# Reordering the first weight chunks of a two-layer diffusion backbone: the first projection chunk before half of the modulation

## What is computed

```python
mod = silu(c) @ w_ada[l] + b_ada[l]                 # 6 x 1024: shift, scale, gate for each half
h = rms_norm(x, norm_g[l, 0]) * (1 + sc_m) + sh_m
q, k, v, u, vm, bg, cg, hx = split(h @ w_in[l])     # 1024 x 2816
y = concat([attention(q, k, v), gating_mlp(u, vm), short_conv(bg, cg, hx)]) @ w_out[l]
x = x + gt_m * rms_norm(y, norm_g[l, 1])
h = rms_norm(x, norm_g[l, 2]) * (1 + sc_f) + sh_f
f = swiglu(h) if l == 0 else moe_swiglu(h)          # layer 1: top 2 of 8 experts
x = x + gt_f * rms_norm(f, norm_g[l, 3])
```

## Time and profile before

| | us |
|---|---|
| median of 3 runs | 1576.52 (1573.6 to 1576.85) |
| the profiled execution's own time | 1577.02 |
| its span, first to last instruction | 1575.2 |
| PE busy (matmul) | 1533.6, 97% of the span |
| DVE busy, ACT busy | 1019.3 (65%), 872.4 (55%) |
| chain that ended last, by engine | PE 89%, DVE 4%, DMA 3%, ACT 2% |

### The profile page before, as it was taken

The page is one execution under the profiler, slowest core; times in us unless marked ns, Lnnn a source line. Parts: engine busy times, 40 slices in busy tenths (PEclk is TensorE's granted clock), DMA queues, the critical chain, the costliest instruction groups (busy, mean ns, idle before and its releaser), DMA issues.

```text
span 1575.2 us, 26693 instructions
## 1 busy us (share of the span) xinstructions
PE 1533.6 (97%) x11239; PEld 1251.7 (79%) x11239; DVE 1019.3 (65%) x943; ACT 872.4 (55%) x889; POOL 178.6 (11%) x196
## 2 busy tenths in 40 slices
PE   5999999999999999999999999999999999999997
PEld 4787788888888888787888888888888878878876
DVE  1437573333323644667888888898888976666667
ACT  2535452222322545546777777777777764654555
POOL 3111100000000400013102030200303000002000
PEclk9999999999999999999999999999999999999999
DMA  9886425667665573145999999999999997778782
GB/s 325 309 278 177 128 82 162 222 222 247 227 244 205 156 237 121 56 158 204 383 384 385 376 376 385 369 379 377 383 377 373 384 360 256 267 277 303 255 331 84
DMA packets 215027, 426.23 MB, mean 271 GB/s; under 512 B 22272, under 2 KB 63520, under 8 KB 214272
## 3 DMA queue, kind: packets, MB, share of 16 engines
q1 hardware_dynamic: 200448, 397.99, 71.1%
q0 software_dynamic: 12640, 19.54, 4.2%
q10 hardware_dynamic: 1808, 6.86, 1.1%
HBM read 419.11 MB, written 20.87 MB: 279 GB/s over the span
## 4 chain that ended last, share of the span: by engine, by line
PE 89%; DVE 4%; DMA 3%; ACT 2%; SPq 1%; issue 0%; ACTq 0%; DVEq 0%
PE ps L1714 25%; PE ps L1716 25%; PE ps L1715 25%; PE ps L2283 3%; PE ps L1755 2%; PE ps L2249 1%; ACT whi L799 1%; PE ps L2316 1%; DVE wlo L1177 1%; DMA raw<-in_w_in_dram 1%; DMA raw<-in_w_ada_dram 1%; DVE x L1268 1%; PE ps L1903 1%; SPq L595 1%; PE ps L1887 1%; PE ps L1872 1%
## 5 line engine op out<-in xcount | busy, mean ns | idle before, releaser
L1177 DVE TENSOR_TENSOR wlo<-raw,whi 128x2048 fp32r<-128x2048 f32 x327 | 746.6, 2291 | 316.3 <-ACT whi L799 262.1
L799 ACT ACTIVATE whi<-raw 128x2048 fp32r<-128x2048 f32 x327 | 626.7, 1918 | 440.0 <-PE ps L1716 200.1
L1714 PE MATMUL ps<-whi,xhi 128*128 128x512 f32 (+1 forms) x1352 | 534.3, 395 | 5.5 <-DVE wlo L1177 5.1
L1716 PE MATMUL ps<-whi,xlo 128*128 128x512 f32 (+1 forms) x1352 | 522.3, 386 | 0.0
L1715 PE MATMUL ps<-wlo,xhi 128*128 128x512 f32 (+1 forms) x1352 | 521.8, 386 | 0.0
L1714 PEld LDWEIGHTS ps<-whi,xhi 128*128 128x128 f32 x1352 | 254.0, 188 | 63.3 <-issue 10.7
L1716 PEld LDWEIGHTS ps<-whi,xlo 128*128 128x128 f32 x1352 | 253.9, 188 | 52.7 <-issue 0.2
L1715 PEld LDWEIGHTS ps<-wlo,xhi 128*128 128x128 f32 x1352 | 254.4, 188 | 47.2
L1714 PE MATMUL ps<-whi,hhi 128*128 128x512 f32 x484 | 192.2, 397 | 0.0
L1716 PE MATMUL ps<-whi,hlo 128*128 128x512 f32 x484 | 188.8, 390 | 0.0
L1715 PE MATMUL ps<-wlo,hhi 128*128 128x512 f32 x484 | 188.6, 390 | 0.0
(11 more groups left out here) (262 smaller groups left out, 1096.9 us busy)
## 6 DMA issues: line engine op xcount, KB each, us to landing
raw<-in_w_moe_gu_dram SPq DMA_DIRECT2D x352, 512.0 KB
raw<-in_w_moe_d_dram SPq DMA_DIRECT2D x176, 512.0 KB
raw<-in_w_ada_dram SPq DMA_DIRECT2D x96, 512.0 KB
raw<-in_w_in_dram SPq DMA_DIRECT2D x44, 512.0 KB
raw<-in_w_ffn_gu_dram SPq DMA_DIRECT2D x44, 512.0 KB
raw<-in_w_ffn_d_dram SPq DMA_DIRECT2D x22, 512.0 KB
raw<-in_w_out_dram SPq DMA_DIRECT2D x16, 512.0 KB
bias<-rpb_rows POOLq DMA_DIRECT2D x32, 96.0 KB, 6.1
```

The source lines that it names most:

```text
L799: act.activation(whi[m % SPL][:, :], raw[n % RING][:, :], ACT.Copy).then_inc(s_hi, 1)
L1177: dve.tensor_tensor(wlo[n % RING][:, :], raw[n % RING][:, :], whi[NTH[n] % SPL][:, :].bitcast(F32), ALU.subtract).then_inc(s_lo, 1)
L1714: pe.matmul(out, a_hi, w_hi, start=start, stop=False)
L1716: return pe.matmul(out, a_lo, w_hi, start=False, stop=stop)
```

## The change

The first pairs go in the order 0, 2, 1, 3, and W6 follows directly behind pair 2, so that the shift and scale of k-tiles 0 to 3 come first. `x` is loaded after two chunks. The columns are made in two halves (`first_columns`), with a semaphore of their own, `s_modh`. On PE the products of pairs 1 and 3 move into W6, behind its first token tile. The later pairs follow W7 (4), W0 (5 and 6), W1 (7), W2 (8), W3 (9). `gvb`, `ws` and `bs` wait in addition until ACT has split W7 (`s_hi` 2); `rpb_rows`, `ck`, `cv` and `wcb` go behind the bias row of pair 6, which waits until DVE has made pair 4's gate. `repeated` moves to another address, and ACT's wait for `s_rows` falls away. The dummy matmuls become 12, 3 and 22 in place of 6, 6, 6, 3 and 8.

Stream order after: pair 0, pair 2; W6; pair 1, pair 3; W7; pair 4; W0; pairs 5, 6; W1; from there as before.

The diff, cut: left out are the renamings by which the first pairs' row buffers, banks and counts go by place (`place_of`) and not by pair.

```diff
-X_AFTER = 4
+X_AFTER = 2
...
-ADA_AFTER = [{p: [HEAD + p] for p in range(MIXER - HEAD)}, {1: [MIXER], 2: [MIXER + 1]}]
+HEAD_ORDER = [0, 2, 1, 3]
+ADA_AFTER = [{1: [4], 2: [5, 6], 3: [7], 4: [8], 5: [9]}, {1: [MIXER], 2: [MIXER + 1]}]
...
-    out = [("ada", 0, j) for j in range(2 * HEAD)]
-    out.insert(2 * HEAD - 2, ("win", 0, WIN_SEQ[0]))
+    out = [("ada", 0, 2 * i + h) for i in HEAD_ORDER for h in range(2)]
+    out.insert(HEAD, ("win", 0, WIN_SEQ[0]))
...
-    return first + 3 if n == first else n if first < n <= first + 2 else n + 1
+    return first + 5 if n == first else n if first < n <= first + 4 else n + 1
...
+def place_of(l, i):
+
+    return HEAD_ORDER.index(i) if l == 0 and i < HEAD else i
...
+        repeated = at("repeated", 48128, [P, 2 * KW * GW])
         qT = at("qT", 33792, [P, 4, NT * P])
...
                     pool.wait_ge(s_tr, KT)
-                    pool.wait_ge(s_rep, 1)
-                    pool.dma_start(rpb_rows.rearrange("l r q j -> (l r) (q j)"),
-                                   repeated[0:7 * NH * DEPTH, :]).then_inc(s_rows, 16)
+                    pool.wait_ge(s_hi, 2)
...
+                else:
+                    brow(l, 6)
+                    pool.wait_ge(s_rep, 1)
+                    pool.dma_start(rpb_rows.rearrange("l r q j -> (l r) (q j)"),
+                                   repeated[0:7 * NH * DEPTH, :]).then_inc(s_rows, 16)
...
-                    for i in range(6, MIXER):
+                    for i in range(7, MIXER):
...
-                upto(n_next)
-                act.wait_ge(s_modc, 2 * l + half + 1)
+                if s == 0:
+                    upto(PLACE["win", 0, WIN_SEQ[0]])
+                else:
+                    upto(n_next)
+                    act.wait_ge(s_modc, 2 * l + half + 1)
                 for kt in range(0, KT, 2 if s == 3 else 1):
+                    if s == 0 and kt == 4:
+                        upto(n_next)
+                    if s == 0 and kt % 4 == 0:
+                        act.wait_ge(s_modh, kt // 4 + 1)
...
-                        if l == 0 and p == 1 and t == 0:
-                            act.wait_ge(s_rows, 16)
...
+
+            def first_columns(h):
+
+                dve.wait_ge(s_colmm, 2 * h + 2)
+                dve.wait_ge(s_gcol, 16 * 2 * DEPTH)
+                k = slice(4 * h, 4 * h + 4)
+                shift, scale = [ps[:, 7, COLUMNS_AT + 16 * i:COLUMNS_AT + 16 * i + 16]
+                                .rearrange("p (k g) -> p k g", g=2)[:, k, :] for i in range(2)]
+                dve.tensor_copy(modc[:, 0, k, :], shift)
+                for g in range(2):
+                    ins = dve.scalar_tensor_tensor(out=modc[:, 1, k, g], in0=scale[:, :, g], scalar=1.0,
+                                                   in1=gcol[:, 0, 0, k], op0=ALU.add, op1=ALU.mult)
+                ins.then_inc(s_modh, 1)
+                if h:
+                    ins = dve.sem_inc(s_modc, 1)
...
+                    if s == 0 and kt == 4:
+                        for i in HEAD_ORDER[2:]:
+                            ada(0, i)
+                        first_columns(1)
+                        upto(PLACE["win", 0, WIN_SEQ[1]])
...
-            for i in range(HEAD):
-                ada(0, i)
-                if i == HEAD - 3:
-                    scaled(0, 0, 0)
-                if i == HEAD - 2:
-                    upto(PLACE["win", 0, WIN_SEQ[0]])
-            mod_columns(0, 0)
+            ada(0, HEAD_ORDER[0])
+            scaled(0, 0, 0)
+            ada(0, HEAD_ORDER[1])
+            first_columns(0)
+            upto(PLACE["win", 0, WIN_SEQ[0]])
...
-                for i in range(HEAD):
-                    if i == 1:
-                        pe.wait_ge(s_const, N_CONST)
-                    if i == HEAD - 1:
-                        for kt in range(4):
-                            turn_x(0, kt)
-                        ada_turn(0, HEAD - 2)
-                        for kt in range(4, KT - 1):
-                            turn_x(0, kt)
-                        warm(6, 4)
-                    ada(0, i)
-                    if 0 < i < HEAD - 1:
-                        ada_turn(0, i - 1)
-                        warm(6, 4)
+                ada(0, HEAD_ORDER[0])
+                pe.wait_ge(s_const, N_CONST)
+                ada_turn(0, HEAD_ORDER[0])
+                warm(12, 4)
+                for kt in range(KT - 1):
+                    turn_x(0, kt)
+                ada(0, HEAD_ORDER[1])
                 warm(3, 4)
-                ada_turn(0, HEAD - 1)
-                warm(8, 4)
+                ada_turn(0, HEAD_ORDER[1])
+                warm(22, 4)
                 turn_x(0, KT - 1)
+
+            def rest_of_head(turn):
+
+                for i in HEAD_ORDER[2:]:
+                    if turn:
+                        ada_turn(0, i)
+                    else:
+                        ada(0, i)
...
+                            if l == 0 and p == 0 and t == 1 and i == 0:
+                                rest_of_head(True)
+                        if l == 0 and p == 0 and t == 0:
+                            rest_of_head(False)
```

More of the change, by code:

```diff
@@ L192, in build @@
         pr = at("pr", 0, [P, NT, D_IN])
-        repeated = at("repeated", 16384, [P, 2 * KW * GW])
+        repeated = at("repeated", 48128, [P, 2 * KW * GW])
         qT = at("qT", 33792, [P, 4, NT * P])
@@ L280, in build @@
         s_modc = sem("s_modc")
+        s_modh = sem("s_modh")
         s_ss = sem("s_ss")
@@ L447, in ada_out @@
             if l == 0 and i < HEAD:
-                return ps[:, 5 + i % 2, NT * P:NT * P + P]
+                return ps[:, 5 + place_of(l, i) % 2, NT * P:NT * P + P]
             return ps[:, 6 if (l, i) in ADA_IN_FFN else 5 + i % 2, 0:P]
@@ L620, in brow @@
             def brow(l, i):
-                if ADA_B * l + i >= 2:
-                    pool.wait_ge(s_modr, ADA_B * l + i - 1)
+                p = place_of(l, i)
+                if ADA_B * l + p >= 2:
+                    pool.wait_ge(s_modr, ADA_B * l + p - 1)
                 for g in range(2):
-                    pool.dma_start(brow_of[g:P:32, i % 2, :],
+                    pool.dma_start(brow_of[g:P:32, p % 2, :],
                                    b_ada[l, 512 * i:512 * i + 512].rearrange("(j n) -> j n", j=4)
-                                   ).then_inc(s_brow[i % 2], 16)
+                                   ).then_inc(s_brow[p % 2], 16)
             def norm_row(l, j):
@@ L637, in _ @@
             chain(pool.memset(grow[:, :, :], 0.0))
-            brow(0, 0)
-            brow(0, 1)
+            brow(0, HEAD_ORDER[0])
+            brow(0, HEAD_ORDER[1])
             const = Chain(pool, s_const)
@@ L695, in _ @@
                 else:
-                    brow(l, 2)
-                    brow(l, 3)
+                    brow(l, HEAD_ORDER[2])
+                    brow(l, HEAD_ORDER[3])
                     norm_row(l, 1)
@@ L1196, in ada @@
             def ada(l, i):
+                p = place_of(l, i)
                 dve.wait_ge(s_pe, done(PLACE["ada", l, 2 * i + 1]))
-                dve.wait_ge(s_brow[i % 2], 32 * (ADA_B // 2 * l + i // 2 + 1))
+                dve.wait_ge(s_brow[p % 2], 32 * (ADA_B // 2 * l + p // 2 + 1))
                 mod, h = divmod(i, 2)
-                row = brow_of[:, i % 2, :]
+                row = brow_of[:, p % 2, :]
                 if mod in (2, 5):
@@ L1211, in ada @@
                 else:
-                    if i >= 2:
-                        dve.wait_ge(s_colmm, turned(ADA_B) * l + turned(i - 2))
-                    dve.tensor_tensor(mrow[:, i % 2, :], ada_out(l, i), row, ALU.add).then_inc(s_modr, 1)
+                    if p >= 2:
+                        dve.wait_ge(s_colmm, turned(ADA_B) * l + turned(p - 2))
+                    dve.tensor_tensor(mrow[:, p % 2, :], ada_out(l, i), row, ALU.add).then_inc(s_modr, 1)
             def mod_columns(l, half):
@@ L1733, in ada_turn @@
                 m = [0, 1, None, 2, 3][mod]
-                pe.wait_ge(s_modr, ADA_B * l + i + 1)
+                p = place_of(l, i)
+                pe.wait_ge(s_modr, ADA_B * l + p + 1)
                 o = COLUMNS_AT + 16 * m + 8 * h
-                pe.matmul(ps[:, 7, o:o + 8], mrow[:, i % 2, :], sel[:, :, :].rearrange("p j g -> p (j g)"),
+                pe.matmul(ps[:, 7, o:o + 8], mrow[:, p % 2, :], sel[:, :, :].rearrange("p j g -> p (j g)"),
                           start=True, stop=True).then_inc(s_colmm, 1)
@@ L1746, in ada @@
                     pe.wait_ge(s_modr, ADA_B * l + i)
-                elif i >= 2:
-                    pe.wait_ge(s_modr, ADA_B * l + i - 1)
+                elif place_of(l, i) >= 2:
+                    pe.wait_ge(s_modr, ADA_B * l + place_of(l, i) - 1)
                 for h in range(2):
```

## The result

| | before | changed kernel |
|---|---|---|
| median of 5 runs of each, us | 1576.52 (1573.6 to 1576.85) | 1585.43 (1582.71 to 1588.51) |
| ratio, 95% interval | | 1.0058 (1.004 to 1.0075) |
| span of the profiled execution | 1575.2 | 1586.8 (its own time 1588.51) |

The change is slower by 8.9 us; 4.6 had been forecast. The sign is right and the size is half of what came. The profiled execution is the slowest of the five, so its trace has some 3 us more than the median. The ratio is worked out from all the runs; it is not the quotient of the two medians, and so the same loss is 8.9 us by the medians and 9.1 by the ratio.

A forecast was written before the change was run, and what follows sets the result against it. PE was taken as the bound, W1's start setting the end. W1 2.3 us later plus one slowed stretch 2.3 made 4.6 on 1577.0: 1581.6, or 1581.1 against the median; range 1576.5 to 1585.5.

The forecast's parts named there:

- Where W1 starts: W1 waits for five chunks (13.6 us) and small loads (4.8) after W0's landing; starts at 81.8, 2.3 later.
- The lead at the head: Head: x and pair 2 earlier, so W6 starts at 33.3 us, 9.7 earlier than before.
- the lead at the head is lost: Rival: half clock during turns, pair 2 and dummies starts W6 3.4 us later; 5.7 in all, 1582.2; chance 0.08.
- The gain kept at W0, faster: Rival: W1's data there by 72.0, PE sets W1's start at 76.3, 3.2 earlier; 1573.3; chance 0.13, 0.07 of it faster.
- The clock at the new pauses: New pauses of 4.3 us before W7 and 5.5 before W1 may bring half clock; taken as 2.3 us.
- one slowed stretch: Half clock behind one of the pauses before W7 and W1, at the mean of the two places, 2.3 us.
- both pauses are answered: Rival: half clock behind the pauses before both W7 and W1; 7.0 us in all, 1583.5; chance 0.10.
- the main case: Late W1 from the small loads' collision, plus half clock behind one new pause: 4.6 us slower; chance 0.47.
- The sum of the head: W1's later start, 2.3 us, plus half clock behind one pause, 2.3: 4.6 us slower.
- whatever moves the start of W1 moves the end by as much: PE is busy 113.05 of 113.50 us from W1's start to 193 us, so only the first 80 us were followed.
- cost 5.1: The 22 dummies in front of W6's last turn take 5.1 us, from 27.8 to 32.9.
- if the time between W1 and 193 us changes: Sign of being wrong: the stretch from W1's start to 193 us was to keep its length.

The follow-up runs named there:

- experiment 1: Also written small_early: changed kernel with the small loads issued early, as before the change, and pair 6's bias row behind them; 1585.62 us, ratio 1.0039.
- after_less8: Changed kernel with 4 dummies in front of W0 in place of 12; 1580.48 us, ratio 1.0031.
- fill_less8: after_less8 with 15 dummies added in front of W7 and 20 in front of W1; 1580.56 us, ratio 1.003.
- before_pad8: Kernel before the change with 20 dummies in front of W0 in place of 12; 1580.06 us, ratio 1.0027.
- before_pad16: Kernel before the change with 28 dummies in front of W0 in place of 12, executed once; 1581.28 us.
- w7_first: Changed kernel with ACT's split of W7 ahead of the fifth k-tile; 1585.8 us, ratio 1.0052.
- small_early_w7_less8: Changed kernel with small loads early, 4 dummies in front of W0 in place of 12, W7's split ahead of the fifth k-tile; 1575.13 us, ratio 0.9991.
- combined: Changed kernel with small loads early, 4 dummies before W0 in place of 12, 6 of W6's 22 dummies moved before W7; 1574.81 us, ratio 0.9992.
- before_pad64: Kernel before the change with 76 dummies in front of W0 in place of 12, executed once; 1585.18 us.

## Why the prediction was right in sign and wrong in size

**Where W1 starts: right.** The mechanism, W1 five chunks behind W0 in the queue and the small loads among them, is what ACT shows; 18.9 us from W0's landing to W1's for 18.4 forecast, 4.9 us for the small loads for 4.8 (experiment 1; 4 to 6 by the other profiles), a pause of 5.56 for 5.5. W1's start was forecast at 81.8: 82.4 in after_less8, 84.6 in the changed kernel's profile.

**The lead at the head: smaller in the profiled run.** W6 was forecast for 33.3 and came at 35.15, because the clock was at 0.50 during the turns (21.0 to 27.8 us). That was the rival "the lead at the head is lost", a chance of 0.08, and it does not exclude the others: in this execution it came together with the late W1. It comes and goes: in the profile of after_less8, of the same head, the 19 turns take 2.29 us.

**The gain kept at W0, faster: not so.** It needed W1 split by 77.7, its data there some 4 us before that (the "about 73" comes to 72 when its terms are added again). W1's data came at 80.35, and at 78.15 and 77.07 in after_less8 and fill_less8.

**The clock at the new pauses: both were answered.** The sum took one slowed stretch at 2.3 us, as a mean of two places; what came, W7's and W1's, is the rival "both pauses are answered", to which 0.10 had been given. The Trainium skill, page "TensorE: Matmul & The Clock Gate", section "Why this matters for your kernels", which was set against the main case, is borne out by after_less8 and fill_less8: 0.50 and 0.50 behind the unfilled pauses, 1.00 and 1.00 with them filled. What W1 lost is 2.7 us, where 3.4 had been set.

**The sum of the head is right in size, in part by luck.** Forecast +4.6. Measured without the 32 instructions: ratio 1.0031, 4.9 us (3.2 to 6.6). The case behind the 4.6 is not the one that came. The rival that did come had 7.0, which is too much: in after_less8 W1 starts 2.9 us late and takes 2.7 us more, 5.6 in all.

**The step that failed is the dummies', with the first part's "So whatever moves the start of W1 moves the end by as much, and I follow the first 80 us".** Of the 22 dummies the prediction said only that they "cost 5.1": their time, and not that they and the other two numbers are eight more than before, which is 32 PE instructions. That term was left out of the sum, and measured alone it is 0.27% (0.17 to 0.38), 4.3 us (before_pad8), with a pause of 2.4 us in the router, one of 2.4 us at the `hx` turns, and a stretch at half clock behind each. 4.9 and 4.3 are 9.2; the change measured 9.1 (1.0058 of 1576.5). Each term is uncertain by 1.7 us, and on small_early the same eight dummies were worth 6.9, so the two add up within the noise, and that they do so to 0.1 us is chance. The prediction said it would be wrong "if the time between W1 and 193 us changes". It hardly does: the difference is 7.2 us at W1's end (95.15 for 79.52 + 8.4) and still 6.6 when the router begins. It changes behind that, where the prediction did not look.

The trace of the kernel before shows no such pause, so no row priced it, and the term was put at nothing without a reason given. What could be seen is the burst of 192 matmuls in the trace and the counts of the dummies in the diff. The range had nothing for it: the median, 1585.43, is at its top of 1585.5, and by the ratio the time is just above it.

**What the late pauses are.** Shown for the router: the place of its pause depends on the number of PE instructions ahead of it. 32 more than in the kernel before give a pause after 191 of the 192 matmuls, in all six profiles that have 32 more; 64 and 140 more give one after 175 and 137; 256 more and none more (five profiles) give none. The steps of 32 and 76 instructions move it by 16 and 38 matmuls, half as many, as each has its load. The Trainium skill, page "Runtime: NRT & Kernel Launch", section "Instruction fetch mechanics", has a rule that fits: an engine's instructions come in blocks of 256, fetched while the block before is worked off.

The traces hold these fetches, as packets of a DMA queue of their own. The page of the kernel before, part 3:

```profile
q8 instruction: 93, 1.52, 0.4%
```

93 packets of 16 KB go with 22478 loads and matmuls of PE, one for 242. In the changed kernel one packet runs from 724.39 to 725.35 us (the view of DMA shows it in 724.35 to 725.40 and none from 723.51 to 729.00 outside that), and PE goes on at 726.75. So it is at every late pause in the router, in the small matmuls behind it and at the `hx` turns: in the eight profiles that have such pauses, PE goes on 2.1 to 2.7 us behind the start of a packet of q8 and 1.2 to 1.4 us behind its end. That the pauses are waits for instructions is read from this.

The Trainium skill's section calls the cost of a boundary mostly hidden; the runs agree for ordinary matmuls, of which most boundaries show no pause, and show 1.6 to 2.6 us at the router, whose 384 instructions take 1.8 us, 1.2 for 256 of them. If the boundary before lies 256 instructions ahead, it is behind the 63rd matmul in the changed kernel, the 47th in before_pad16 and the 9th in fill_less8, and the pause ends 3.2, 3.2 and 2.8 us behind it; 3.6 in before_pad8 and 3.8 in w7_first. PE gets through the 256 in less than that. But the second pause of before_pad16 doesn't follow this: PE goes on at 721.29, the next packet starts only at 725.39. What sets off a fetch stays open.

The `hx` turns stall in the six profiles with 32 more, and not with 0, 64, 140 or 256. But two of the five profiles with none more (small_early_w7_less8 and combined) have a pause of 3.4 us some 5 us ahead of those turns, at the entry of the same part of the program. Two packets of q8 are fetched there in quick succession, at 1294.32 and 1295.88 in the one, both at 1292.1 in the other. What decides at this place stays open.

## What to carry to other kernels

Idle work on an engine has two prices, the time where it stands and the place of every instruction behind it: count the instructions that a change adds to an engine, and look for bursts of short ones far behind. A pause with the releaser "issue" in a burst, in one kernel and not in the other, is the sign, and the DMA queue of kind "instruction" shows whether a fetch lies in it. Moving it away can be cheap (eight dummies fewer took the changed kernel from 1.0058 to 1.0031 of the kernel before). And when the first buffers are freed earlier but the queue has the same bytes to bring by the third chunk, nothing is won: put the small loads where the weight queue waits, not where it is full.

## What had not been expected of the hardware

- 32 instructions of no use, early on PE, cost 4.3 us far behind (before_pad8); 256 brought neither late pause (before_pad64, one execution).
- PE stands until 1.2 to 1.4 us behind the end of a fetch of 16 KB of its instructions, in a burst that needs 1.2 us for 256 of them.
- A pause of 5.8 us ahead of one chunk cost 2.7 us more through the clock, and dummies in it, at no time of their own, kept it (81.5 to 88.0 us: 0.50 without, 1.00 with).
- The clock in the turns of the head is at 0.50 in one execution (19 turns, 4.32 us) and at full rate in another of the same code (2.29 us). Differences of 2 us at the head between single profiles mean nothing by themselves.
